# Scan stage of a hybrid decoder layer: right sides issued in groups, first inverse evicted ahead of them, last pair products moved into the corner's gap, masked and diagonal copies reordered

## What is computed

```python
def hgrn2_mixer(...):           # called A here
    scores = einsum('bhtd,bhsd,bhtsd->bhts', qc, kc, exp(cum_t - cum_s))   # s <= t
    out = scores @ vc + (qc * exp(cum)) @ state
    state = exp(last) * state + (kc * exp(last - cum)).T @ vc

def rwkv7_mixer(...):           # called D here
    sa = einsum('bhij,bhj->bhi', state, -kkt)
    state = state * wt + sa[..., None] * (kkt * at) + vt[..., None] * kt
    y = einsum('bhij,bhj->bhi', state, rt)
```

## Time and profile before

| | |
|---|---|
| median of three runs | 3721.41 us |
| the profiled execution | 3717.61 us |
| its span, first to last instruction | 3715.4 us |
| PE busy over the span | 90% |
| DVE, ACT, POOL busy | 55%, 35%, 13% |
| mean granted TensorE clock | 0.94 of full speed |

### The profile page before, as it was taken

The page is one execution under the profiler, slowest core; times in us unless marked ns, Lnnn a source line. Parts: engine busy times, 40 slices in busy tenths (PEclk is TensorE's granted clock), DMA queues, the critical chain, the costliest instruction groups (busy, mean ns, idle before and its releaser), DMA issues. The chain is left out here.

```text
span 3715.4 us, 55067 instructions
## 1 busy us (share of the span) xinstructions
PE 3342.3 (90%) x21296; PEld 2717.4 (73%) x21296; DVE 2037.0 (55%) x3083; ACT 1297.7 (35%) x1944; POOL 488.3 (13%) x650
## 2 busy tenths in 40 slices
PE   6998988499996858989999969999999999999998
PEld 4766766388885846876788858877787788777876
DVE  4656565445545747724444437744774476536752
ACT  3644545244442022211323324423442244234422
POOL 2332333355651001100000000000000000000000
PEclk9999999688887978989999979999999999999999
DMA  3252542312111014433121132234222422333232
GB/s 125 76 174 76 172 146 76 120 53 70 54 53 45 1 47 168 158 127 122 34 68 62 57 113 91 91 107 142 99 93 102 138 100 99 99 123 120 90 103 90
DMA packets 163546, 360.97 MB, mean 97 GB/s; under 512 B 11057, under 2 KB 95281, under 8 KB 151345
## 3 DMA queue, kind: packets, MB, share of 16 engines
q1 hardware_dynamic: 163376, 358.53, 28.7%
HBM read 287.18 MB, written 71.30 MB: 96 GB/s over the span
## 5 line engine op out<-in xcount | busy, mean ns | idle before, releaser
L2386 PE MATMUL ffn_ps<-ffn_hn_high,w_ring_high 128*128 128x512 f32 x1408 | 557.4, 396 | 30.4 <-DVE w_ring_low L2485 27.8
L2386 PE MATMUL ffn_ps<-ffn_hn_high,w_ring_low 128*128 128x512 f32 x1408 | 556.5, 395 | 0.0
L2386 PE MATMUL ffn_ps<-ffn_hn_low,w_ring_high 128*128 128x512 f32 x1408 | 556.5, 395 | 0.0
L2485 DVE TENSOR_TENSOR w_ring_low<-w_ring_raw,w_ring_high 128x2048 fp32r<-128x2048 f32 (+1 forms) x176 | 309.4, 1758 | 353.1 <-ACT w_ring_high L2419 342.6
L2419 ACT ACTIVATE w_ring_high<-w_ring_raw 128x2048 fp32r<-128x2048 f32 (+1 forms) x176 | 261.1, 1484 | 376.1 <-PE ffn_ps L2401 331.4
L2386 PEld LDWEIGHTS ffn_ps<-ffn_hn_high,w_ring_high 128*128 128x128 f32 x1408 | 265.9, 189 | 95.5 <-issue 33.4
L365 PE MATMUL proj<-hn_high,w_high 128*128 128x512 f32 x672 | 280.7, 418 | 36.0 <-POOL w_low L292 36.0
L2386 PEld LDWEIGHTS ffn_ps<-ffn_hn_high,w_ring_low 128*128 128x128 f32 x1408 | 265.8, 189 | 62.1
L2386 PEld LDWEIGHTS ffn_ps<-ffn_hn_low,w_ring_high 128*128 128x128 f32 x1408 | 266.0, 189 | 61.7
L2401 PE MATMUL ffn_ps<-w_ring_high,hidden_high 128*128 128x512 f32 x704 | 280.2, 398 | 11.6 <-DVE w_ring_low L2485 6.2
L2401 PE MATMUL ffn_ps<-w_ring_low,hidden_high 128*128 128x512 f32 x704 | 279.0, 396 | 0.0
(11 more groups left out here) (446 smaller groups left out, 6327.6 us busy)
## 6 DMA issues: line engine op xcount, KB each, us to landing
w_ring_raw<-in_w_up SPq DMA_DIRECT2D x88, 1024.0 KB, 4.8
w_ring_raw<-in_w_down SPq DMA_DIRECT2D x88, 512.0 KB, 3.5
w_ring<-in_w_feat SPq DMA_DIRECT2D x84, 512.0 KB, 3.6
feats<-scratch_scan SPq DMA_DIRECT2D x16, 896.0 KB, 4.4
x_t<-in_x SPq DMA_DIRECT2D x4, 2048.0 KB, 8.0
m_x<-in_x SPq DMA_DIRECT2D x16, 512.0 KB, 3.5
scratch_h<-m_x SPq DMA_DIRECT2D x16, 512.0 KB, 3.1
xa_ring<-in_wkv SPq DMA_DIRECT2D x16, 512.0 KB, 3.6
```

The costliest lines, as they stand in the source:

```text
L2386: mm = pe.matmul(ps[:, 2 * u + g], w[a][:, u, g * D_MODEL + k * P:g * D_MODEL + (k + 1) * P], hn[b][:, k], start=k == a == b == 0, stop=k ...
L2485: dve.tensor_tensor(dst, loads[:, u, 0:n], high_part, ALU.subtract).then_inc(split.sem, 1)
```

## The change

In the scan alone, with the same instructions in number and kind:

- ACT evicts the first inverse (both halves) before it waits for the right sides, where it did so after.
- PE issues the right sides as four products with 128 rows, then four with 64 rows, where they alternated. The first product of each bank carries the start flag.
- PE issues the last two groups of pair products after `triangles`, ahead of `corner_times`, where they stood ahead of `off_times(n, 4)`.
- DVE does `corner_y` and `start_inverse` before the copy and the three masked copies of the last pair products, where they came after. `prepare_qk` moves from the end of the call to behind `multiply(0)` of the next, for the same chunk.
- ACT's diagonal copies move from the end of the call to the next call, behind the eviction of level 0.
- PE waits for `qk_ready` before the first pair products, because their signal lets the loads overwrite what `prepare_qk` reads.

```diff
--- before.py
+++ after.py
@@ -860,14 +860,14 @@
             def run(i, k, u, steps, has_b):
                 n, v = i + 1, 1 - u
                 has_a, has_prep = steps > 0, steps > 1
+                if has_a:
+                    for g in range(2):
+                        act.wait_ge(*x0_done.at(n, g))
+                        act.activation(invs[:, g, 0].rearrange("p t n -> p (t n)"), ps_g[:, g, P:2 * P], ACT.Copy).then_inc(x0_out.sem, 1)
                 if has_b:
                     act.wait_ge(*rhs_done.at(i))
                     act.activation(rhs[:].rearrange("p (q t) n -> p q (t n)", q=2), ps_t[:, :, 2 * G2 * HD:3 * G2 * HD], ACT.Copy,
                                    scale=-1.0).then_inc(rhs_ready.sem, 1)
-                if has_a:
-                    for g in range(2):
-                        act.wait_ge(*x0_done.at(n, g))
-                        act.activation(invs[:, g, 0].rearrange("p t n -> p (t n)"), ps_g[:, g, P:2 * P], ACT.Copy).then_inc(x0_out.sem, 1)
                 if has_b:
                     act.wait_ge(*sa_done.at(i))
                     act.activation(sa[:].rearrange("p h n -> p (h n)"), ps_t[:, 1, 0:H * HD], ACT.Copy).then_inc(sa_ready.sem, 1)
@@ -876,6 +876,11 @@
                         for g in range(2):
                             act.wait_ge(*x_done.at(n, 2 * level + g))
                             act.activation(invs[:, g].rearrange("p a t n -> p (a t n)"), ps_g[:, g, P:3 * P], ACT.Copy).then_inc(x_out.sem, 1)
+                    if level == 0 and has_b:
+                        act.wait_ge(*scored_a.at(i, 1))
+                        for j in range(2):
+                            last = act.activation(scores_a[u][rows(j), :, rows(j)], diag_a[rows(j)], ACT.Copy)
+                        last.then_inc(diag_out.sem, 1)
                     if level == 0 and has_prep:
                         exp_halves(i + 2, u, 0)
                     if level == 1 and has_b:
@@ -904,10 +909,6 @@
                     act.wait_ge(*cx_done.at(n))
                     act.activation(inv[v][0:HD, :, HD:].rearrange("p (g t) n -> p g t n", g=2),
                                    ps_g[0:HD, :, P:2 * P].rearrange("p g (t n) -> p g t n", t=G2), ACT.Copy, scale=-1.0).then_inc(cx_out.sem, 1)
-                    act.wait_ge(*scored_a.at(n, 1))
-                    for j in range(2):
-                        last = act.activation(scores_a[v][rows(j), :, rows(j)], diag_a[rows(j)], ACT.Copy)
-                    last.then_inc(diag_out.sem, 1)
 
             act.wait_ge(*loaded[0].at(0))
             prepare_d(0, 0)
@@ -1005,6 +1006,7 @@
                     kind(v, KPK, 0)
                     kind(v, BR, G2 * TC)
                     multiply(0)
+                    prepare_qk(n, v)
                     hold(*kinds_done.at(n, 1))
                     kind(v, KPR, 0)
                     multiply(1)
@@ -1028,6 +1030,11 @@
                     prepare_kr(i + 2, u)
                 if has_a:
                     multiply(4)
+                    dve.wait_ge(*cy_done.at(n))
+                    dve.tensor_copy(corner_y[HD:].rearrange("p (g t) n -> p g (t n)", g=2), ps_g[HD:, :, 0:P]).then_inc(cy_out.sem, 1)
+                if has_prep:
+                    start_inverse(n + 1)
+                if has_a:
                     dve.wait_ge(*pairs_a.at(n, 1))
                     dve.tensor_copy(scores_a[v][0:HD, :, HD:].rearrange("p (q t) n -> p q t n", q=2),
                                     ps_q[0:HD, :, 3 * P:].rearrange("p q (t n) -> p q t n", t=G2))
@@ -1035,16 +1042,10 @@
                     wait_own(me, pick(me, 3, 0))
                     wait_own(me, pick(me, 4, 1))
                     pick(me, 5, 2).then_inc(scored_a.sem, 1)
-                    dve.wait_ge(*cy_done.at(n))
-                    dve.tensor_copy(corner_y[HD:].rearrange("p (g t) n -> p g (t n)", g=2), ps_g[HD:, :, 0:P]).then_inc(cy_out.sem, 1)
-                if has_prep:
-                    start_inverse(n + 1)
-                    prepare_qk(i + 2, u)
 
             prepare_mid(0, 0, 0)
             prepare_kr(0, 0)
             start_inverse(0)
-            prepare_qk(0, 0)
             iterations(run)
 
         @block.tensor
@@ -1141,11 +1142,16 @@
                 hold(states.at(i, back=1))
                 hold(v_loaded[u].at(k))
                 hold(kinds_out.at(i))
+                def to(q, t):
+                    return ps_t[:, q, 2 * P + t * HD:2 * P + (t + 1) * HD]
+
                 for t in range(G2):
                     for q in range(2):
-                        to = ps_t[:, q, 2 * P + t * HD:2 * P + (t + 1) * HD]
-                        pe.matmul(to, scores_d[u][:, KPK, slot(q, t)], vd[u][:, head(q, t)], start=True, stop=False)
-                        mm = pe.matmul(to, kr[u][rows(q), t, 0], state_d[u][rows(q), t], start=False, stop=True)
+                        pe.matmul(to(q, t), scores_d[u][:, KPK, slot(q, t)], vd[u][:, head(q, t)], start=t == 0, stop=False,
+                                  skip_group_check=True)
+                for t in range(G2):
+                    for q in range(2):
+                        mm = pe.matmul(to(q, t), kr[u][rows(q), t, 0], state_d[u][rows(q), t], start=False, stop=True, skip_group_check=True)
                 mm.then_inc(rhs_done.sem, 1)
 
             def solved(i, u):
@@ -1211,6 +1217,7 @@
                     off_times(n, 1)
                     hold(halves_ready.at(n))
                     hold(scored_a.at(n - 1, 1)) if has_b else None
+                    hold(qk_ready.at(n))
                     pairs(v, None, 0).then_inc(raw_used.sem, 1)
                     pairs(v, 6, 1)
                     new_inverse(n, 1)
@@ -1237,12 +1244,12 @@
                     pairs(v, 3, 0)
                     pairs(v, 2, 1)
                     new_inverse(n, 3)
-                    pairs(v, 1, 2)
-                    pairs(v, 0, 3).then_inc(pairs_a.sem, 1)
                     off_times(n, 4)
                     new_inverse(n, 4)
                     if has_prep:
                         triangles(n + 1, u)
+                    pairs(v, 1, 2)
+                    pairs(v, 0, 3).then_inc(pairs_a.sem, 1)
                     corner_times(n)
                     corner_inverse(n, v)
                 if has_prep:
```

## The result

The changed kernel takes 3639.04 us (median; 3632.41 to 3640.12), the one before 3721.37: ratio 0.9774, 95% interval 0.9757 to 0.9791. It is 82 us faster where 55 were forecast and 77 stood at the end of the range. The profiled execution took 3640.12 us, its span is 3637.8; against the profiled execution of before (3717.61) that is 77.5 us, and the other 5 are the distance of the two profiled executions from their medians.

A forecast was written before the change was run, and what follows sets the result against it. PE's own instruction list, its few waits and its clock were taken as the bound. Path 30 plus clock 25 made 55 us: 3717.6 to 3662.6 profiled, 3666 as median; range 3650 to 3682, over the cases 3644 to 3692.

The forecast's parts named there:

- the clock's term: Behind the right sides: TensorE's clock holds in most chunks instead of falling; two thirds of 37 us, 25 us gained.
- Right sides and ACT's order: Right sides and the wait behind them: grouping gains 1.20 us, evicting the first inverse ahead 0.65; 1.85 us a chunk.
- rival 3: Right sides: 128-row products don't overlap each other's weight loads, only the 64-row group gains; 7 us less, 3673; chance 0.08.
- DVE's order: Reordered DVE copies and prepare_qk cost nothing, bounds 0 and 0.5; w is ready 0.6 us before PE wants it.
- Rival 4: DVE's copies take double beside POOL, PE waits about 2 us for w and the 1.85 is used up; 3717; chance 0.05.
- Pair products in the gap: Corner: moving the last pair products into PE's idle time behind triangles gains nothing, bounds 0 and 0.1.
- a rival for the slower side: Corner: the clock falls there as well in each chunk, 25 us slower, 3746; chance 0.03.
- Rival 2: Scan: the clock never falls; 30 + 41 = 71 us gained, 3650; chance 0.12.

The follow-up runs named there:

- no_act_order: The changed kernel with ACT evicting the right sides before the first inverse again, as in the kernel before; 3671.08 us, ratio 0.9864.
- before_filled: The kernel before with 12 unused matmuls added where PE waits for ACT behind the right sides; 3711.71 us, ratio 0.9972.
- pairs_back: The changed kernel with only the last two groups of pair products moved back ahead of off_times(n, 4); 3664.05 us, ratio 0.9839.
- groups_and_act: The kernel before with only the right sides in groups and the first inverse evicted ahead; 3666.08 us, ratio 0.9859.
- pairs_moved_alone: The kernel before with grouped right sides, first inverse evicted ahead and pair products moved; DVE's order and ACT's diagonal copies stay old; 3689.27 us, ratio 0.9921.
- no_groups: The changed kernel with the right sides alternating between 128-row and 64-row products again; 3697.9 us, ratio 0.9938.
- no_act_filled: The changed kernel with ACT's evictions in the old order and 12 unused matmuls in the hole behind the right sides; 3650.39 us, ratio 0.9809.
- both_again: Repeat of the changed kernel with the inverse's lower block copied first, corner_times waiting for fewer copies, and the second exponential moved to level 1; 3635.46 us (first run 3633.87).

## Why the prediction was wrong

The direction and the kind of effect stood, the size did not. The step that failed is the clock's term: two thirds of 37 us, 25, were taken for what measured 45. By its steps:

- *Right sides and ACT's order: right, somewhat low.* 1.85 us a chunk were summed up; it is 24.72 - 22.63 = 2.09 between chunks at full clock, 31 us in 15. Of the 2.08 from right sides to `off_times`, the hole is 0.81 (0.65 forecast) and the groups 1.27 (1.20). The first group costs 1.04 for an estimated 1.0, the second 0.59 instead of 0.78.
- *Loads of 128 rows don't overlap (rival 3): wrong.* Eight records in 1.10 us, one lasting 0.28.
- *DVE's order at nothing, `w` in time by 0.6 us: right to the tenth.* Rival 4 fell with the copies at 1.38 and 1.34. `prepare_qk` never held PE back.
- *Pair products in the gap at nothing, bounds 0 and 0.1.* On the path that is what they are worth (22.62 against 22.63). But nothing was put down for what their place does to the clock. I looked at the corner only as a place where the clock had held, and put the one chunk where it had fallen into a rival for the slower side. With the right sides in groups and the products in their old place, the clock falls in the corner in nine chunks of 16; with them in the gap it doesn't: 25 us.
- *The clock's term, the step that failed: 25 us for 45.* Two things were wrong in it. A third of the 37 was struck off for falls that would remain behind the right sides; none remained before the last chunk, there or in the corner, and the runs show that this takes both things: dense right sides with the hole closed or filled, and the pair products in the gap. And the whole was larger than 37: the low clock took 7.8 us a chunk, not the 6.9 of the chunk I had read, since some chunks had 10 or more. Its price is (27.73 - 24.72) / 7.8 = 0.39 us for each us at 1.2 GHz, against 2.5 / 6.9 = 0.36 forecast. The other runs give 0.41 (no_act_order), 0.43 (before_filled), 0.47 (pairs_back), 0.48 (groups_and_act) and 0.40 (pairs_moved_alone); these are a little high, since the mean chunk of the changed kernel is 0.1 us above its shortest with no low clock at all. So 3.0 us a chunk, 45 in 15.
- That groups_and_act, the change without its corner part, measured the forecast 3666 is luck: its clock falls in the corner, where the forecast expected none.
- Rival 2, the clock that never falls, is what happened. It said 71 us, and the two profiled executions are 77.5 apart: 4 more from the clock (45 against 41), the rest from the path. The other 5 of its 11 us are the distance of the profiled executions from their medians.

Path 31 and clock 45 make 76 us; it is 75 between the first and last right sides, since the changed kernel's mean chunk is 22.73 and not 22.63. The first chunk begins 4 us earlier, and behind the last right sides about 1 us is lost again, which gives the 77.5 of the profiled executions.

## What to carry over

Price a reordering twice, once on the path and once by what it does to the clock, and for the second look for the next thinnest stretch, not only for the one you mend: edits of 0 us on the path were worth 25 here, and the parts' gains don't add up. Each against the kernel before in its own comparison, the groups alone gave 35 us, with ACT's order 53, with the corner 82; but taking only the groups out of the changed kernel lost 59. The chunk whose clock never falls gives the path's length; a run with idle holes filled by unused matmuls shows it cheaply.

## What the runs showed of the hardware

- The clock of TensorE fell behind a stretch in which the engine was busy 3.00 us of 3.00, and 3.70 of the 3.70 that followed (no_groups), and was held by unused matmuls in a hole of 0.8 us (no_act_filled: 1.00 against 0.92). The Trainium skill, TensorE: Matmul & The Clock Gate, in its table on why this matters for kernels, advises to avoid long idle gaps between bursts so that the clock doesn't drop. The trace disagrees with that as a sufficient rule: no_groups had no gap there at all, and in the corner ahead only those of 0.52 us and less that the changed kernel has too.
- A change between products with 128 rows and with 64 rows of weights costs about 0.2 us at 2.4 GHz: 1.27 us for the six changes fewer. In the alternating order of before each product starts 0.36 us after the last, whichever way the shape changes (881.38, 881.74 and then 882.11), though only every second one adds to the place just written, so it is not that. The Trainium skill, TensorEngine Tiling (Array Packing), Tiling Modes, says that changing the tiling mode drains the engine; the trace agrees.
- Of two operations of 128x256 on DVE beside POOL, the masked copy out of PSUM took 0.46 us (1.38 for three) and `first_off`, with both inputs in SBUF, 0.95. With POOL idle, four such copies took 1.88 us in the kernel before, 0.47 each, and the product that makes `kr`, of the same size and with both inputs in SBUF, 0.42.
- A DVE operation on 128x2 elements that takes 0.155 us lasted 5.37 beside twelve products of POOL in a row, until the last of them ended (both_again; 5.36 in both).
